# The closing products of a decoder step: norms and the 22-tile product cut into units of one block

## The reference, cut to what matters

```
u = rmsnorm(h);  q_a, kv_a, q_idx, k_idx, w_idx, q_b, k_b, v_b, g_a, g_b = split(u @ w_in)
# branch A: an indexer scores each key, the 256 best are attended to (grouped heads)
score[t,s] = sum_h w[t,h] * relu(q_idx[t,h] . k_idx[s]);  sel = top_k(score, topk)
# branch B: differential attention over all keys
a = softmax(q1 k1^T) - lam * softmax(q2 k2^T);  o_b = rmsnorm(a @ v) * (1 - lam_init)

def layer_out(h, o_a, o_b, g_a, g_b, p_i, tail):          # the "closing products"
    merged = sigmoid(g_a) * (o_a @ w_br_a) + sigmoid(g_b) * (o_b @ w_br_b)
    h = h + rmsnorm(merged @ w_out, attn_post_g)           # norm 1
    gate, up = split(rmsnorm(h, ffn_pre_g) @ w_gate_up)    # norm 2
    h = h + rmsnorm((silu(gate) * up) @ w_down, ffn_post_g)  # norm 3
    return h + sigmoid(h @ w_ple_gate) * (p_i @ w_ple_proj)
```

## Time and profile before

| | us |
|---|---|
| median of 3 runs | 3674.64 |
| lowest and highest | 3669.53, 3682.44 |
| profiled execution, own time | 3671.66 |
| its span in the trace | 3670.1 |
| sample_select, with its products | 1091.5 to 1621.4 |
| sample_attend, with its products | 1623.0 to 3416.0 |
| last tail | 3419.1 to 3667 |
| PE busy, whole span | 2985.0 |
| PE idle before value matmuls for their load (L1710) | 77.2 |

### The profile page before, as it was taken

The page is one execution under the profiler, slowest core; times in us unless marked ns, Lnnn a source line. Parts: engine busy times, 40 slices in busy tenths (PEclk is TensorE's granted clock), DMA queues, the critical chain, the costliest instruction groups (busy, mean ns, idle before and its releaser), DMA issues. The chain is left out here.

```text
span 3670.1 us, 69563 instructions
## 1 busy us (share of the span) xinstructions
PE 2985.0 (81%) x26553; PEld 2081.3 (57%) x26553; DVE 1547.9 (42%) x3004; ACT 587.1 (16%) x1294; POOL 589.5 (16%) x1089
## 2 busy tenths in 40 slices
PE   8999899548959688647698988888778989878697
PEld 4444366336749588644465655555545555545596
DVE  2222389837743677543643332253444333102211
ACT  1111210026634200000110110010111010101101
...
GB/s 193 85 99 81 105 58 77 55 130 1 1 62 231 95 132 133 106 162 188 215 267 303 296 285 267 290 305 295 278 288 230 305 267 302 186 205 123 160 264 153
...
## 3 DMA queue, kind: packets, MB, share of 16 engines
...
...
## 5 line engine op out<-in xcount | busy, mean ns | idle before, releaser
L975 PE MATMUL sa_t<-tw_z,tw_w 128*128 128x352 f32 x1664 | 546.4, 484 | 19.0 <-DVE tw_x L1069 10.1
L1808 DVE STREAM_TRANSPOSE sa_key_b<-sa_ring_k 128x2048 f32<-128x2048 f32 x128 | 294.3, 2306 | 456.4 <-PE sa_s L1647 244.7
L1573 POOL DMA_DIRECT2D sa_ring_v<-cache_b_kv x512 | 275.6, 538 | 1097.2 <-PE sa_o L1714 738.6
L975 PEld LDWEIGHTS sa_t<-tw_z,tw_w 128*128 128x128 f32 x1664 | 323.7, 199 | 213.0 <-issue 55.6
L975 PE MATMUL sa_t<-tw_x,tw_w 128*128 128x352 f32 x960 | 310.4, 483 | 53.1 <-DMA tw_w<-w_br_a 45.7
L213 PE MATMUL pr_acc<-pr_w,pr_u_t 128*128 128x512 f32 (+1 forms) x864 | 326.6, 539 | 0.0
L1574 POOL DMA_DIRECT2D sa_ring_va<-cache_a_kv x512 | 275.0, 537 | 53.7 <-issue 24.9
L975 PEld LDWEIGHTS sa_t<-tw_x,tw_w 128*128 128x128 f32 x960 | 188.6, 200 | 163.5 <-issue 68.6
L213 PEld LDWEIGHTS pr_acc<-pr_w,pr_u_t 128*128 128x128 f32 x864 | 152.2, 190 | 167.9 <-issue 167.9
L1647 PE MATMUL sa_s<-sa_key_b,sa_q_pad 32*32 32x256 f32 x8192 | 195.7, 423 | 45.1 <-DVE sa_key_b L1808 41.3
L439 PE MATMUL sel_g<-sel_u,sel_gw 128*128 128x352 f32 x768 | 228.8, 461 | 0.0
...
## 6 DMA issues: line engine op xcount, KB each, us to landing
...
```

Of the source, the lines that this page charges most:

```text
L975: ins = pe.matmul(bank[:, 0:self.width], self.w[:, at % self.SLOTS, k - lo, :], moving[:, k, :], start=(k == 0), stop=(k == kc - 1))
L1573: pool.dma_start(ring_v[:, n % RING, :], rows_of(cache_b, page, 1)).then_inc(v_in[n // 4 % 2], 16)
L1808: nc.vector.transpose(key_b[:, at:at + 4].rearrange("p g n s -> p (g n s)"), ring_k[:, at:at + 4, :].rearrange("p g e -> p (g e)")).then_i ...
```

## The change

The units become smaller. A norm's unit n1, n2 or n3 now holds only its statistics, and eight units a1, a2 or a3 follow, one for each block of 128 rows; they have no part on PE, take no bank and no `done`. In each a1 and a3 unit DVE drains once more than before. The unit dn becomes three, d0, d1 and dn (8, 8 and 6 k-tiles), which go on in one bank but have their own `done` and their own load; a load is issued four blocks ahead of each. The four first weight loads of a Tail are issued between o_t and the gates. The planner's costs follow (what an is_last unit of a product costs extra falls from 4.0 to 2.5), and in sample_select the slot bias has a weight of 20 of its own. In sample_attend the transposition of the mask on PE and its copy on DVE stand in the slot of the first scores instead of ahead of everything.

```
 class Tail:
-    KINDS = {"ma": ("w_br_a", 0, 4), ..., "dn": ("w_down", 0, 22), ...}
+    KINDS = {"ma": ("w_br_a", 0, 0, 4), ...,
+             "d0": ("w_down", 0, 0, 8), "d1": ("w_down", 0, 8, 16), "dn": ("w_down", 0, 16, 22), ...}
...
-        one = ... [("wo", n) for n in range(KC)] + [("n1", 0), ("n2", 0)]
-        one += [(kind, n) for n in range(self.F_TILES) for kind in ("gg", "up")] + [("dn", n) for n in range(KC)] + [("n3", 0)]
+        one = ... [("wo", n) for n in range(KC)] + [("n1", 0)] + [("a1", k) for k in range(KC)]
+        one += [("n2", 0)] + [("a2", k) for k in range(KC)]
+        one += [(kind, n) for n in range(self.F_TILES) for kind in ("gg", "up")] + [(kind, n) for n in range(KC) for kind in ("d0", "d1", "dn")]
+        one += [("n3", 0)] + [("a3", k) for k in range(KC)]
...
+            if kind[0] != "a":
+                counted += 1
+                self.done_by[g], self.bank_of[g] = counted, banked
+                banked += kind not in ("d0", "d1")
...
     def cost(self, g):
         p, kind, n = self.units[g]
+        scale = self.width / 352
         if kind in self.KINDS:
-            return self.width / 587 * self.KINDS[kind][2] + (4.0 if self.is_last(g) else 0.0)
-        return {"n1": 13.0, "n2": 8.0, "n3": 8.0, "yt": 1.0}[kind] * self.width / 352 + 1.0
+            return 0.6 * scale * (self.KINDS[kind][3] - self.KINDS[kind][2]) + (2.5 if self.is_last(g) else 0.0)
+        return {"n1": 4.5, "n2": 4.5, "n3": 4.5, "yt": 1.0, "a1": 1.8, "a2": 0.7, "a3": 1.2}[kind] * scale
...
     def load_inputs(self, sp, p):
         sp.dma_start(self.o, ...)
+        if p == 0:
+            for at in range(self.SLOTS):
+                self.load_weights(sp, at)
         sp.dma_start(self.gates, ...)
...
     def sync(self, sp, g):
         if kind in self.KINDS:
-            sp.wait_ge(self.done, g + 1)
-            for at in range(self.first[g], self.first[g + 1]):
-                if at + self.SLOTS < len(self.loads):
-                    self.load_weights(sp, at + self.SLOTS)
+            sp.wait_ge(self.done, self.done_by[g])
+            if self.load_of[g] + self.SLOTS < len(self.loads):
+                self.load_weights(sp, self.load_of[g] + self.SLOTS)
...
     def vector(self, dve, g):
-            for k in range(KC):
-                ...
+        if kind in ("a1", "a2", "a3"):
+            gain = self.gains[:, int(kind[1]) - 1, n:n + 1]
+            if kind == "a2":
+                nc.vector.scalar_tensor_tensor(out=self.z[:, n], in0=self.h[:, n], scalar=gain, in1=self.rstd[:], ...).then_inc(self.normed, 1)
+                return
+            src = (self.u if kind == "a1" else self.z)[:, n]
+            dve.drain()
+            nc.vector.scalar_tensor_tensor(out=self.sig[:, n % 2], in0=src, scalar=gain, in1=self.rstd[:], ...)
+            dve.drain()
+            nc.vector.tensor_tensor(self.h[:, n], self.h[:, n], self.sig[:, n % 2], ALU.add).then_inc(...)
+            if kind == "a1" and n:
+                self.add_square(dve, self.of_square(p, "n1", n - 1))
...
 def sample_select(nc, a):
-    BY_GROUP, BY_COUNT = 0.5, 8.0
+    BY_GROUP, BY_COUNT, BY_RANK, BY_BIAS = 0.4, 7.5, 16.0, 20.0
...
 def sample_attend(nc, a):                                # on PE; DVE's copy moves alike
-            pe.wait_ge(mask_set, 1)
-            pe.transpose(stat[:, 0:NQ], mask_t[:], ident[0:NQ, 0:NQ]).then_inc(stat_done, 1)
             pe.wait_ge(consts, 1)
             for slot in order:
                 if slot == ("scores", 0):
+                    pe.wait_ge(mask_set, 1)
+                    pe.transpose(stat[:, 0:NQ], mask_t[:], ident[0:NQ, 0:NQ]).then_inc(stat_done, 1)
                     pe.wait_ge(small_in, 33 * 16)
```

148 lines of the change are left out of this document (72 added, 76 removed).

## The result

The changed kernel took 3575.14 us in the median of 4 runs (3570.4 to 3589.23), the kernel before, beside it, 3672.09 (3669.37 to 3682.44). The ratio is 0.9733, with a 95% interval of 0.9702 to 0.9764: faster by 2.4 to 3.0%. Forecast were 3603, −72 us; measured are −97. In a second measurement it took 3577.23 (ratio 0.9727, 0.9698 to 0.9756).

A forecast was written before the change was run, and what follows sets the result against it. TensorE, busy 81% of the span, was taken as the bound, its idle time the gain. Last tail −13, sample_attend −42 and sample_select −17 gave −72 on 3671.7, 3599.7, plus 3.0 for the median: 3603 us, range 3568 to 3655.

The forecast's parts named there:

- Last tail's w_down: Last tail: each load follows its own block, 61.2 to 46.5 us, less +2 for drains; −13, bounds −19.7 to −9.
- sample_select, −17: Whole phase: start −6, count 0 earlier −6, between counts −35, after count 32 +29; bounds −32 to +5.
- the walk between counts: sample_select's 32 periods between counts, summed from blocks and norms in the changed order: 309 against 344 us, −35.
- sample_attend, −42: Whole phase: fewer value waits in both w_down stretches, norm 1 −8, n3's drains +2; bounds −65 to 0.
- the first w_down: sample_attend, 2200 to 2520, DMA at .90: value waits of 23 us covered by w_down pieces, half counted, −12.
- The second w_down: sample_attend, 3133 to 3354, DMA at .57: three value waits in full and 5 us of two others, −24.6.
- norm 1: sample_attend, both pieces: DVE turns keys between the norm's blocks; 5.5 and 6.5 us, of which 8 counted.
- B: sample_attend: value waits come back as slower landings where DMA is at .90; −52.6, 3622 us; chance .22.
- C: Slow matmuls behind each wait go too, at some fifteen places: 20 us more, 3583 us; chance .12.
- A: The forecast itself, whole kernel: 3603 us, without counting any gain from the clock; chance .54.
- D: sample_select's end gives back +46, sample_attend wins only the second w_down stretch: 3664 us, no change; chance .07.
- E: sample_attend: SyncE, strictly in order, issues key loads later behind the split units; +11, 3686 us; chance .05.

The follow-up runs named there:

- s_884: The changed kernel with eight weight slots instead of four beside sample_select and in the last tail: 3567.10 us.
- t_dn_loads: The changed kernel with the loads behind a w_down product all asked for after its third piece, as before the change: 3613.17 us.
- u_gates: The changed kernel with the gates' load issued ahead of the first four weight loads again: 3581.57 us.
- u_select: The changed kernel with sample_select's planner weights as before the change (dots 0.5, update 8, rank 16, bias 0): 3582.14 us.
- t_norms: The changed kernel with each norm's eight block units directly behind its statistics, for all three norms: 3587.81 us.
- t_dn_place: The changed kernel with the three pieces of a w_down product side by side, each keeping its own early load: 3621.80 us.
- t_dn_both: The changed kernel with w_down pieces side by side and their loads asked for after the third piece: 3642.69 us.
- a_again: The changed kernel measured once more, unaltered, to show how its phases vary: 3577.23 us.

## Why the prediction was right, and what was mis-sized

**Last tail's w_down, −13 forecast.** Right in mechanism, mis-sized at both ends. The forecast took 61.2 us before and 46.5 after. But 3570.5 is where the first wait begins and not where w_down begins: the 352 matmuls took 66.4 us, and take 43.4 now, −23.0 against −14.7. The lower bound of 41.5 (352 matmuls at .118) was not reached; s_884 with its eight slots takes 40.9. The 16 drains cost what was reckoned, some 2 us: VectorE's eight blocks take 9.58 us where they took 8.67 in norm 1, and 6.52 where they took 5.26 in norm 3. Up to norm 1 the phase is 2.4 us longer (49.8 for 47.4), although TensorE's first product comes 3.7 us sooner; no run explains that. Phase −18 in the first profile, −14 to −18 over seven of the same code. t_dn_loads gives it all back.

**First weights.** Right: nothing in the last tail and sample_attend, 6 us in sample_select (u_gates: 5.7).

**sample_select, −17.** Right by its total, −14 and −11 in the two profiles, and its parts hit −12, −35 and +29 within 3 us. In the walk between counts one term does not add up: ten periods of 9.65 and seven of 7.65 with 4.6 for flushes are 154.7 us and not 158.5, and the sum is 305 and not 309. The trace has 158.0 there, so the hit on this term has luck in it. And two of the reasons that stand behind these numbers fell. The three parts are not three gains: u_select moves 24 us from one to the other with no effect on the sum. And the norms' split, which the walk had as its first item, is worth nothing here (t_norms −4 to −7). The sum consists of 6 us by the gates' order and 7 to 10 by the loads of w_down, 2 to 5 by its pieces' places; norms and weights come to about nothing. A walk through the order tells when things happen; it does not tell which edit is the cause.

**sample_attend, −42.** The mechanism was right and two terms were mis-sized, the larger one at the first w_down: "In 2200 to 2520, with DMA at .90, the like come to 23; the refill may then land later instead, so I count half, −12." By the steps 24 to 40, which hold the same work, it is −27.8, and t_dn_place and t_dn_both give all of it back (399.0 and 398.7, where the eleven kernels with the pieces apart have 368.3 to 372.6). The waits for the values' loads themselves fell by about the 12 that were counted, from 22.1 us to 9.5. As much again went with them that had no term: idle time that other releasers ended, 6.7 us of it VectorE's tile sa_top and 4.3 the next piece's first weights. t_dn_place has 22.4 us for the values again, and the rest at other waits than before (8.4 at VectorE's tile sa_o_row), so which small wait goes depends on the order, and that was not tried apart. The second w_down was sized well: −19.1 behind the last scores with a block of 5 us more in it, so some −24, against −24.6 +2; waits of 3.42 and 3.35 us at 3102 and 3107 stayed, which stand ahead of w_down; t_dn_place gives back 14 to 16 of it by one profile. By the medians the place of the pieces is worth 40 to 45 us of sample_attend (+45 to +47, less sample_select's 2 to 5), against the 36.6 forecast.

The other term is norm 1, "5.5 and 6.5, of which I count 8". From wo7 to gate 0 it was 9.1 and 8.2 us. Over a longer stretch nothing is left at the first piece: steps 0 to 24 take 496.9 us where they took 496.7, with waits for values of 16.2 us where there were 8.7. At the second, steps 40 to 48 are 17.7 shorter with a block of 5 fewer, so some 13. So norm 1 gave some 13 against 8, and all at the second piece. t_norms costs more, 23 us there and 4 in steps 0 to 24 (by the whole phase 12 to 29, against the kernels with the changed one's sample_attend; by the medians some 15 to 20, with sample_select's 4 to 7 added), but its order has a wait of 20.09 us that the kernel before did not have, and it glues all three norms: it shows what norms in one piece would cost the changed kernel, not what the change won with them. The working of the first piece's walk can't be followed: eight blocks of 1.71, three steps of 2 and three turns of 2.3 us are 27 and not 39; measured were 35.7.

**Signs that were named.** Held: the granted clock of the last tail's w_down (1.00), no wait over 10 us for key_b (7.08 and 8.38), the end of sample_select with w_ple_proj behind sel_rows. Missed: the value matmuls' waits came down to 50 us and not to 40; two transfers of w_down are left in the chain; one period between counts is 17.73 us, where none was to be over 16; the last count comes 43 us earlier and not 50. DMA's share, for which "over .95 in 2200 to 2520" would have been a sign of being wrong, stands at .95 in 2133 to 2450 and at .96 in steps 24 to 40, with the time shorter all the same: it was no sign of that.

**Rivals.** B said that the values would land later where DMA stands at .90, and had 0 for the first w_down stretch. It doesn't hold: DMA went up and the stretch lost 27.8 us. Of its waits for values 9.5 of 22.1 us did stay. The Trainium skill says on its page DMA: Bandwidth & Descriptors, "Issuing engines are not separate DMA queues", that all issuing engines share 16 DMA engines; that is not against it, but sharing did not mean that the shared engines were the limit. C said that slow matmuls behind waits would go too, and its 3583 is the nearest of the five to the 3575 measured; yet its mechanism has only a part. TensorE's busy time in the whole of sample_attend, 18959 matmuls in each, fell from 1479.9 us to 1474.1, and to 1464.4 in a_again: 6 to 16 us, with a granted clock of .90 before and .91 and .92 after. In the last tail w_down's busy time rose by 7.1 when its waits came back. Granted clock 1.00 in the tail's w_down stretch against .89 agrees with the section "HAM oscillation — how this bites in real kernels" of the Trainium skill's page TensorE: Matmul & The Clock Gate. I had named it and left it out of A. D and E did not come: the end of sample_select came as reckoned, and VectorE waits less for keys, not more.

**What stays open.** The forecast was short by 25 us. By the profiles, sample_attend gave 24 of them (16 in steps 24 to 40, 5 at the norms, 4 in steps 48 to the last, which are no more than scatter) and the last tail 5; sample_select and the phases before it took some 5 back. Of the 16 us next to nothing is clock, since TensorE's busy time in steps 24 to 40 fell by 2.0 us only; which of the smaller waits go with the pieces, and why, stays open. The new costs of the planner were not tried apart; all the kernels here that come after the change have them.
